# A chunkwise mLSTM scan: stabiliser rows brought in by DMA instead of by TensorE, one minimum for four heads

## The chip, the cores and the metric

The kernel runs on one core of one Trainium2 chip. The metric is the device time of one execution in microseconds (us); the median of three runs of the kernel before is 2629.45 us.

## The reference, cut to what matters

The program is a two-layer encoder trunk (attention and a Hyena operator, then a bidirectional mLSTM, each followed by a mixture of experts) on 1024 positions of width 1024, all in float32. The change lies in the mLSTM of the second layer. It has 4 heads, a forward and a backward scan, chunks of 128 positions; q and k have 128 components a head, v has 256.

```python
def step(carry, inp):                       # one chunk of one head and direction
    c_st, n_st, m_st = carry
    qj, kj, vj, lij, lfj = inp
    bcum = jnp.cumsum(lfj, axis=-1)
    dmat = bcum[..., :, None] - bcum[..., None, :] + lij[..., None, :]
    dmat = jnp.where(mask, dmat, -jnp.inf)
    inter = bcum + m_st[..., None]
    m_t = jnp.maximum(inter, jnp.max(dmat, axis=-1))
    w_intra = jnp.exp(dmat - m_t[..., None])
    w_inter = jnp.exp(inter - m_t)
    sc = jnp.einsum('bgtd,bgsd->bgts', qj, kj) * w_intra
    num = (w_inter[..., None] * jnp.einsum('bgtd,bgde->bgte', qj, c_st)
           + jnp.einsum('bgts,bgse->bgte', sc, vj))
    den = w_inter * jnp.einsum('bgtd,bgd->bgt', qj, n_st) + jnp.sum(sc, axis=-1)
    h = num / jnp.maximum(jnp.abs(den), jnp.exp(-m_t))[..., None]
    ...                                     # the state c, n, m is carried on with kw
```

With A = log_i - bcum (one value per source position s) and M the running maximum of A within the chunk and of the carried one, dmat - m_t is A[s] - M[t]: a column plus a row, masked.

## The kernel before, in words

Every stage of the program ("phase") is a block in which each engine has its own instruction list, with counting semaphores between them, and a barrier of all engines at its end. Four stages matter here.

`ml_gates` (from line 2582) projects the output gate in 16 steps of 24 matmuls on TensorE, and beside that works out the gate rows: 36 partitions (forward heads in rows 0 to 3, backward ones in rows 32 to 35, already reversed in time), 1024 positions. Its `turn_rows` (line 2626) turns five such rows (A, WI, ENM, KW and NEGM = -M) into columns with 40 small transposes, `finish` reverses the backward ones with a matmul against a flip matrix (line 2632), and VectorE copies them to `cols` and `colb`. `ml_project_qk` (line 2773) projects q and k. Weights come in chunks of 2 MB into a ring of three slots in SBUF (`refill`, `load_chunk`), issued by SyncE (SP) when a slot is free; `ml_project_qk` loads the last chunk of the output projection and then the first expert's matrix, chunk S_MOE1.

`ml_scan` (from line 2877) goes through 64 units: 8 chunks, in each 4 forward and then 4 backward heads. For chunk index c > 0 the carried state takes part; the first 32 units also compute and keep k.q, which the second 32 reuse (the other direction needs the same products); the first 56 update the state; units 32 on add their result to what the other direction stored. In the order of the engines' lists, for unit u:

- TensorE, `scores(u+2)`: k.q (line 2917, only u < 32); then the row -M spread over all 128 partitions, as a matmul of the broadcast column `col(4)` with the identity (line 2919); then the inter-chunk product of q with the state (line 2925), into one bank, QB. `values(u)`: the weighted scores with v (line 2934) and the keys with v for the state (line 2940). Each is one float32 matmul, which the profile shows as two.
- ScalarE: `inter(u+1)` scales the inter-chunk product into `t1`, of three buffers (line 2969); the copy of k.q (line 2990); the exponential (line 2993); `scaled(u-4)` divides by the denominator (line 2977).
- VectorE: `exponent(u+1)` takes the spread row, adds the column A and bounds by the mask's table (0 where allowed, -1e30 elsewhere), line 3034; `weigh(u)` multiplies the exponential by k.q (line 3044); `finish(u-1)` adds the two products (line 3059, 3062 in chunk 0), updates the state (line 3066, 3071) and, for an odd unit, makes the denominators of two heads with three tiny instructions (lines 3079, 3082, 3088).
- GpSimd: `kw(u)` scales the keys (line 3016); the addition to the stored result (line 3007).

The waits that set this order:

```python
if u >= 3:                                   # scores(u): three banks
    pe.wait_ge(e_ok, u - 2)
    if u - 3 < FIRST:
        pe.wait_ge(kept, u - 2)
...
if u - 2 * MH >= 3:                          # inter(u), three buffers t1
    act.wait_ge(num_ok, u - 2)
...
for u in range(UNITS):                       # VectorE
    if u + 1 < UNITS:
        exponent(u + 1)
    weigh(u)
    if u:
        finish(u - 1)
```

Before the first unit the keys of all chunks are turned by TensorE, and ScalarE and VectorE copy them out by turns (lines 2983, 3092). After the scan comes the output projection with the router (`out_route`).

Of the kernel before, what the change touches and what calls it, by code (L numbers as in the profile page):

```python
# [7 lines left out]
F32 = mybir.dt.float32  # L8
F32R = mybir.dt.float32r
I32 = mybir.dt.int32  # L10
ALU = mybir.AluOpType
# [3 lines left out]
P = 128  # L15
D = 1024
T = 1024
NT = T // P
# [58 lines left out]
def build(nc, I, out):  # L77
    ctx = ExitStack()
    with ctx:
# [38 lines left out]
        so_d = nc.dram_tensor("sigmoid_o_scratch", (T, D), F32).ap()  # L118

# [2462 lines left out]
        def ml_gates(xnH, cols, colb, apr):  # L2582

            (proj, evac, staged0, staged1, w_high, w_rest, w_used,
             bias_in, shifted, sized, expd, logd, ready, powered, turned, moved, flipped, diag_ok,
             chain) = take(19)
            staged = (staged0, staged1)
            with ExitStack() as st:
# [23 lines left out]
                with nc.Block() as block:  # L2612
                    @block.sync
                    def _(sp):
                        sp.dma_start(gb[:], I["ml_gate_b"]).then_inc(bias_in, 16)
                        refill(sp, C0, C0 + CHUNKS, proj, NT)

                    @block.tensor
                    def _(pe):
                        def turn_rows():  # L2620
                            pe.wait_ge(powered, 3)
                            pe.wait_ge(ready, 1)
                            for n in range(5 * NT):
                                q, c = divmod(n, NT)
                                row = (A, WI, ENM, KW, NEGM)[q]
# [4 lines left out]
                        def finish():  # L2630
                            pe.wait_ge(moved, 3)
                            nc.tensor.matmul(psum[:, 7, 0:160], flip[:], cols[:, :, :, 32:36],
# [65 lines left out]
                    def _(dve):  # L2698
# [50 lines left out]
                        V.tensor_scalar(NEGM, M, -1.0, None, ALU.mult).then_inc(ready, 1)  # L2749
# [7 lines left out]
                        for b in range(3):  # L2757
                            n = min(14, 5 * NT - 14 * b) * GROWS
# [4 lines left out]
                        step(V.tensor_copy(colb[:], psum[:, 7, 0:160].rearrange("p (q c h) -> p q c h", q=5, c=NT)))  # L2763
# [113 lines left out]
        def ml_scan(qkT, kn, vA, cols, colb, apr, hs):  # L2877
            (s_ok, qc_ok, v_ok, cc_ok, e_ok, w_ok, scw_ok, t_ok, num_ok, h_ok, c_ok, kw_ok, den_ok,
             chain, recip_ok, kept, scaled_ok, added_ok, k_turned, k_lo, k_hi) = take(21)
            with ExitStack() as st:  # L2880
                C = sb(st, "ml_state", [P, 2 * MH, MVA])
                small = sb(st, "ml_small", [P, 4, 2, P])
                e0, wT, scw, kw = (small[:, n] for n in range(4))
# [6 lines left out]
                SB, QB = (0, 1, 3), 2  # L2890
# [14 lines left out]
                with nc.Block() as block:  # L2905
                    @block.tensor
                    def _(pe):
                        def scores(u):
                            c, d, h, gi, n, col = unit(u)
                            b = SB[u % 3]  # L2910
# [357 lines left out]
```

## Time and profile before

| | us |
|---|---|
| runs | 2629.45, 2623.35, 2631.92; median 2629.45 |
| profiled execution | 2623.78 |
| its span, first to last instruction | 2622.0 |
| busy over the span | TensorE 91%, VectorE 70%, ScalarE 55%, GpSimd 18% |
| `ml_scan` in it | about 1713.2 to 1831.9, 118.7 us or 4.5% of the span |

A row of the timeline gives start, duration, engine, line, operation, what it writes and reads, its shape and how many instructions were merged; in brackets, how long the engine had been idle before and what ended that. PE is TensorE, PEld its loading of weights, DVE VectorE, ACT ScalarE, POOL GpSimd, SPq the queue of SyncE. Names are those of the allocated tiles: `ml_small` holds exponent, weights, weighted scores and scaled keys, `ml_inter` is t1, `ml_num` num, `ml_state` the state, `ml_kq` the kept products, `ml_k` the turned keys, `ml_den` the denominators.

### The profile page before, as it was taken

To read this page: it belongs to the slowest core of one execution; us is meant where nothing else is said; L and a number is where in the kernel's file an instruction comes from. 1 tells how busy PE (TensorE), PEld (TensorE's weight loads), DVE (VectorE), ACT (ScalarE), POOL (GpSimd) and SP (SyncE) were. 2 spreads that over 40 slices of the span, in tenths; PEclk is the share of its full clock that TensorE was granted. 3 is DMA by queue.
4 is the path that set the end of the run, shared out by engine and by line. 5 is a ranking of instruction groups with operands and counts; after the bars stand their busy time and mean duration, and the time that the engine had idled before them with its cause. 6 is when DMAs were issued, how large, how long until landed. Compare 5 with 4: busy or idle time off the path is not lost. (4 is left out here: it accounts for less than half of the span.)

```text
span 2622.0 us, 32575 instructions
## 1 busy us (share of the span) xinstructions
PE 2392.4 (91%) x11612; PEld 1966.8 (75%) x11612; DVE 1826.0 (70%) x2101; ACT 1452.5 (55%) x1777; POOL 482.4 (18%) x431
## 2 busy tenths in 40 slices
PE   7989989796978999999986998988896999999996
PEld 6768877585867888888875876876785888888884
DVE  6848856578447988998963141378637989888982
ACT  6438842322217887888863241256424878877872
POOL 0001100100002333333320000036201333323321
PEclk9989999897988999999997999999897999999999
DMA  5110011111237999999993121000425999999996
GB/s 178 47 52 1 1 48 37 73 33 35 112 124 286 392 380 382 391 388 382 388 382 124 59 84 59 33 33 8 159 108 209 381 382 379 364 386 373 385 389 246
DMA packets 85913, 542.32 MB, mean 207 GB/s; under 512 B 18997, under 2 KB 22678, under 8 KB 59831
## 3 DMA queue, kind: packets, MB, share of 16 engines
q1 hardware_dynamic: 64358, 502.93, 48.9%
q0 software_dynamic: 19008, 33.61, 5.2%
q10 hardware_dynamic: 2448, 4.46, 0.5%
q8 instruction: 62, 1.02, 0.2%
q14 instruction: 37, 0.30, 0.0%
HBM read 521.52 MB, written 55.05 MB: 220 GB/s over the span
## 5 line engine op out<-in xcount | busy, mean ns | idle before, releaser
L2280 DVE TENSOR_TENSOR wL<-ring,wH 128x2048 fp32r<-128x2048 f32 x384 | 869.4, 2288 | 134.5 <-ACT wH L2216 128.2
L2216 ACT CAST wH<-ring 128x2048 fp32r<-128x2048 f32 x384 | 730.1, 1911 | 194.2 <-DMA ring<-in_moe_w 138.7
L2102 PE MATMUL psum<-wH,xgH 128*128 128x512 f32 x1024 | 407.6, 398 | 14.4 <-DVE xgL L2280 14.4
L2104 PE MATMUL psum<-wH,xgL 128*128 128x512 f32 x1024 | 401.2, 392 | 0.0
L2110 PE MATMUL psum<-wL,xgH 128*128 128x512 f32 x1024 | 275.8, 391 | 0.0
L2102 PEld LDWEIGHTS psum<-wH,xgH 128*128 128x128 f32 x1024 | 193.5, 189 | 57.1 <-DVE xgL L2280 13.1
L2110 PEld LDWEIGHTS psum<-wL,xgH 128*128 128x128 f32 x1024 | 193.2, 189 | 40.8
L2104 PEld LDWEIGHTS psum<-wH,xgL 128*128 128x128 f32 x1024 | 193.7, 189 | 38.4
L2102 PE MATMUL psum<-wH,hidH 128*128 128x512 f32 x512 | 206.0, 402 | 3.9 <-DVE hidL L2280 3.9
L2104 PE MATMUL psum<-wH,hidL 128*128 128x512 f32 x512 | 200.2, 391 | 0.0
L2020 POOL COPY gidx<-slots 128x1 int32 (+1 forms) x60 | 61.1, 1019 | 497.5 <-PE psum L2119 497.5
L2110 PE MATMUL psum<-wL,hidH 128*128 128x512 f32 x512 | 137.7, 391 | 0.0
L200 PE MATMUL psum<-xn_high,ring_rest 128*128 128x512 f32 x320 | 127.2, 397 | 0.0
L198 PE MATMUL psum<-w_high_route_rest,y_high_route 128*128 128x512 f32 x256 | 105.7, 413 | 12.6 <-DVE ring_rest L193 12.1
L2102 PEld LDWEIGHTS psum<-wH,hidH 128*128 128x128 f32 x512 | 96.5, 189 | 23.2 <-DVE hidL L2280 4.4
L2110 PEld LDWEIGHTS psum<-wL,hidH 128*128 128x128 f32 x512 | 96.7, 189 | 20.2
L2104 PEld LDWEIGHTS psum<-wH,hidL 128*128 128x128 f32 x512 | 96.7, 189 | 18.3
L2034 POOL COPY yidx<-slots 128x1 int32 (+1 forms) x64 | 97.1, 1517 | 56.9 <-DMA out<-y,yidx 33.6
L199 PE MATMUL psum<-ring_rest,y_high_route 128*128 128x512 f32 x256 | 102.4, 400 | 0.0
L200 PE MATMUL psum<-w_high_route_rest,y_rest_route 128*128 128x512 f32 x256 | 102.1, 399 | 0.0
L199 PE MATMUL psum<-ring_rest,xn_high 128*128 128x512 f32 x256 | 102.1, 399 | 0.0
L2227 ACT ACTIVATE y<-psum,slot_gate 128x1024 f32<-128x1024 f32 x64 | 71.5, 1117 | 49.2 <-PE psum L2110 49.0
(429 smaller groups left out, 4657.3 us busy)
## 6 DMA issues: line engine op xcount, KB each, us to landing
ring<-in_moe_w SPq DMA_DIRECT2D x192, 2048.0 KB
ring<-in_ev_w_in SPq DMA_DIRECT2D x6, 2048.0 KB
xnT<-in_moe_w SPq DMA_DIRECT2D x6, 2048.0 KB, 14.3
ring<-in_od_w_in SPq DMA_DIRECT2D x6, 2048.0 KB
xn_scratch<-xn_route SPq DMA_DIRECT2D x16, 512.0 KB, 2.6
ow<-in_moe_w SPq DMA_DIRECT2D x3, 2048.0 KB, 22.8
v_att<-in_x SPq DMA_DIRECT2D x8, 512.0 KB, 3.9
ring<-in_ev_w_out SPq DMA_DIRECT2D x2, 2048.0 KB
```

The lines of the kernel that those rows point to most:

```text
L198: nc.tensor.matmul(dst, lhs[0], rhs[0], start=start, stop=False)
L199: nc.tensor.matmul(dst, lhs[0], rhs[1], start=False, stop=False)
L200: return nc.tensor.matmul(dst, lhs[1], rhs[0], start=False, stop=stop)
L2020: nc.gpsimd.tensor_copy(idx[:, b:b + 1], slots[:, bass.ds(e, 1)]).then_inc(idx_ok, 1)
L2034: nc.gpsimd.tensor_copy(yidx[:, b:b + 1], slots[:, bass.ds(e, 1)]).then_inc(yidx_ok, 1)
L2102: nc.tensor.matmul(psum[:, bank, :], xh[:, k, :], w3[0][:, n, cols], start=(half == 0 and n == 0), stop=False)
L2104: nc.tensor.matmul(psum[:, bank, :], xl[:, k, :], w3[0][:, n, cols], start=False, stop=False)
L2110: ins = nc.tensor.matmul(psum[:, bank, :], xh[:, k, :], w3[1][:, n, cols], start=False, stop=(half == 1 and n == len(ks) - 1))
L2216: nc.scalar.copy(half_of(wH, b, e, c, half), raw(e, c, half)).then_inc(w_high, 1)
L2227: nc.scalar.activation(y[:, b, :], psum[:, 5:7, :].rearrange("p a b -> p (a b)"), ACT.Copy, scale=slot_gate[:, bass.ds(e, 1)]).then_inc(y_ ...
L2280: return nc.vector.tensor_tensor(out, whole, high.bitcast(F32), ALU.subtract)
```

## The change

The spread row no longer comes from TensorE. `ml_gates` turns four rows instead of five (32 transposes, and 128 columns instead of 160 in the flip matmul); VectorE writes the backward rows of -M once more, reversed, and SyncE stores the 8 rows to a DRAM scratch. In `ml_scan` SyncE reads them back, per chunk and direction 4 heads by 128 positions broadcast to 128 partitions (256 KB in SBUF), 16 such transfers into two buffers that lie in ring slot S_MOE1 % 3; the load of chunk S_MOE1 moves from the end of `ml_project_qk` to the scan, behind the last use of the rows. VectorE takes one minimum of four heads' rows against the mask's table (now +1e30 where allowed), with both inputs in SBUF, once for four units; ScalarE adds the column A as the bias of its exponential. The k.q product has two banks instead of three, the inter-chunk product two instead of one.

```diff
@@ ml_gates
-                        refill(sp, C0, C0 + CHUNKS, proj, NT)
+                        refill(sp, C0, C0 + CHUNKS - 1, proj, NT)
+                        sp.wait_ge(natural, 2)
+                        sp.dma_start(rows_d[0:MH, :], NEGM[0:MH, :]).then_inc(rows_out, 16)
+                        sp.dma_start(rows_d[MH:2 * MH, :], A[32:32 + MH, :]).then_inc(rows_out, 16)
+                        sp.wait_ge(proj, NT * CHUNKS)
+                        load_chunk(sp, C0 + CHUNKS - 1 + RING)
+                        sp.wait_ge(rows_out, 32)
...
-                            for n in range(5 * NT):
+                            for n in range(4 * NT):
...
+                        dve.wait_ge(natural, 1)
+                        V.tensor_copy(A[32:32 + MH, :], NEGM[32:32 + MH, ::-1]).then_inc(natural, 1)
@@ ml_project_qk
-                        refill(sp, C0, C0 + 2, proj, 4)
+                        refill(sp, C0, C0 + 1, proj, 4)
@@ ml_scan
-                SB, QB = (0, 1, 3), 2
+                SB, QB = (0, 1), (2, 3)
+                wide_rows = ring[:, S_MOE1 % RING, 0:4 * MH * P].rearrange("p (b g t) -> p b g t", b=2, g=2 * MH)
...
+                    @block.sync
+                    def _(sp):
+                        for c in range(NT):
+                            if c >= 2:
+                                sp.wait_ge(e_ok, 2 * (c - 1))
+                            for d in range(2):
+                                n = NT - 1 - c if d else c
+                                sp.dma_start(wide_rows[:, c % 2, MH * d:MH * d + MH, :],
+                                             rows_d[MH * d:MH * d + MH, n * P:(n + 1) * P].partition_broadcast(P)
+                                             ).then_inc(rows_in[c % 2], 16)
+                        sp.wait_ge(e_ok, 2 * NT)
+                        load_chunk(sp, S_MOE1)
...
-                            if u >= 3:
-                                pe.wait_ge(e_ok, u - 2)
-                                if u - 3 < FIRST:
-                                    pe.wait_ge(kept, u - 2)
                             if u < FIRST:
-                                nc.tensor.matmul(psum[:, b, 0:P], qkT[:, 4 + h, t], qkT[:, h, t], start=True, stop=True)
-
-                            nc.tensor.matmul(psum[:, b, P:2 * P], col(4).broadcast_to([P, P]), ident[:],
-                                             start=True, stop=True).then_inc(s_ok, 1)
+                                if u >= 2:
+                                    pe.wait_ge(kept, u - 1)
+                                nc.tensor.matmul(psum[:, SB[u % 2], 0:P], qkT[:, 4 + h, t], qkT[:, h, t], start=True,
+                                                 stop=True).then_inc(s_ok, 1)
                             if c:
                                 pe.wait_ge(c_ok, u - 2 * MH + 1)
-                                if u - 2 * MH >= 1:
-                                    pe.wait_ge(t_ok, u - 2 * MH)
+                                if u - 2 * MH >= 2:
+                                    pe.wait_ge(t_ok, u - 2 * MH - 1)
...
-                            act.wait_ge(e_ok, u + 1)
                             if u < FIRST:
+                                act.wait_ge(s_ok, u + 1)
+                                nc.scalar.copy(kq[:, n, h, :], psum[:, SB[u % 2], 0:P]).then_inc(kept, 1)
+                            act.wait_ge(e_ok, u // MH + 1)
                             if u >= 2:
                                 act.wait_ge(scw_ok, u - 1)
-                            nc.scalar.activation(wT[:, u % 2, :], e0[:, u % 2, :], ACT.Exp).then_inc(w_ok, 1)
+                            nc.scalar.activation(wT[:, u % 2, :], e0[:, (u // MH) % 2, h, :], ACT.Exp, bias=col(0)
+                                                 ).then_inc(w_ok, 1)
...
+                        def bound(g):
+                            c, d = divmod(g, 2)
+                            dve.wait_ge(rows_in[c % 2], 32 * (c // 2 + 1))
+                            if g >= 2:
+                                dve.wait_ge(w_ok, MH * (g - 1))
+                            V.tensor_tensor(e0[:, g % 2, :, :], wide_rows[:, c % 2, MH * d:MH * d + MH, :],
+                                            (cap_b if d else cap_f)[:].unsqueeze(1).broadcast_to([P, MH, P]), ALU.min
+                                            ).then_inc(e_ok, 1)
...
+                        bound(0)
                         for m in range(1, NT, 2):
                             dve.wait_ge(k_turned, m + 1)
                             V.tensor_copy(kn[:, key_chunk(m), :], psum[:, 4 + m % 4, :]).then_inc(k_hi, 1)
-                        exponent(0)
                         for u in range(UNITS):
-                            if u + 1 < UNITS:
-                                exponent(u + 1)
+                            if u % MH == 1 and u + MH < UNITS:
+                                bound(u // MH + 1)
                             weigh(u)
```

## Rows read from the trace of the kernel before

**Rows 1.** By stretch: length, busy PE, PEld, DVE, ACT, POOL; clock, DMA share, GB/s.

```profile
1722.00:1736.00 14.00, 13.27 (x78) 12.14 (x79) 12.05 (x48) 7.83 (x29) 5.21 (x9) 1.00 0.01 2
1736.00:1782.00 46.00, 46.00 (x257) 40.76 (x256) 39.23 (x147) 32.31 (x104) 18.70 (x27) 1.00 0.00 1
1782.00:1816.00 34.00, 33.43 (x166) 27.01 (x165) 31.82 (x113) 21.79 (x61) 25.91 (x40) 1.00 0.01 2
```

**Rows 2.** Waits in the last of these stretches: who waited for whom, us, times, longest.

```profile
ACT ml_inter L2969 <- DVE ml_num L3059: 8.1, 10, 1.3
```

**Rows 3.** Timeline of two units of chunk 2, parts of it.

```profile
1758.78 0.60 PE L2925 MATMUL psum<-ml_state,ml_qkT 128*128 128x257 f32 x2
...
1759.42 0.48 ACT L2969 ACTIVATE ml_inter<-psum,ml_cols 128x257 f32<-128x257 f32 x1 [0.51 <-PE psum L2925]
...
1759.79 0.26 ACT L2990 COPY ml_kq<-psum 128x128 f32<-128x128 f32 x1
...
1760.30 0.39 PE L2919 MATMUL psum<-ident,ml_cols 128*128 128x128 f32 x2
...
1760.53 0.60 PE L2925 MATMUL psum<-ml_state,ml_qkT 128*128 128x257 f32 x2
...
1762.04 0.29 DVE L3044 SCALAR_TENSOR_TENSOR ml_small<-ml_kq,ml_small 128x128 f32<-128x128 f32 x1 [0.47 <-ACT ml_small L2993]
...
1763.44 0.35 DVE L3034 SCALAR_TENSOR_TENSOR ml_small<-psum,ml_cols,cap_f 128x128 f32<-128x128 f32 x1
```

**Rows 4.** Timeline of two units of chunk 5, parts of it.

```profile
1797.55 0.28 DVE L3044 SCALAR_TENSOR_TENSOR ml_small<-ml_kq,ml_small 128x128 f32<-128x128 f32 x1
...
1798.26 0.48 ACT L2969 ACTIVATE ml_inter<-psum,ml_colb 128x257 f32<-128x257 f32 x1 [0.80 <-DVE ml_num L3059]
...
1798.97 0.29 DVE L3044 SCALAR_TENSOR_TENSOR ml_small<-ml_kq,ml_small 128x128 f32<-128x128 f32 x1
...
1800.52 0.35 DVE L3034 SCALAR_TENSOR_TENSOR ml_small<-psum,ml_cols,cap_f 128x128 f32<-128x128 f32 x1
...
1800.79 0.28 DVE L3044 SCALAR_TENSOR_TENSOR ml_small<-ml_kq,ml_small 128x128 f32<-128x128 f32 x1
```

**Rows 5.** Timeline of VectorE: the weighing of units 8, 32 and 56.

```profile
1734.04 0.29 DVE L3044 SCALAR_TENSOR_TENSOR ml_small<-ml_kq,ml_small 128x128 f32<-128x128 f32 x1 [0.53 <-ACT ml_small L2993]
...
1775.86 0.29 DVE L3044 SCALAR_TENSOR_TENSOR ml_small<-ml_kq,ml_small 128x128 f32<-128x128 f32 x1
...
1815.33 0.29 DVE L3044 SCALAR_TENSOR_TENSOR ml_small<-ml_kq,ml_small 128x128 f32<-128x128 f32 x1
```

**Rows 6.** One VectorE instruction of `ml_gates` with two SBUF inputs (ns least/median/most).

```profile
L2736 DVE TENSOR_TENSOR gate_rows<-gate_rows x1: 1216/1216/1216, 1527.4 to 1527.4; 36x1024 f32<-36x1024 f32 x1
```

**Rows 7.** Groups of ScalarE instructions without and with a per-partition operand, 512 elements.

```profile
L1605 ACT ACTIVATE hy_abs<-xnT 128x512 f32<-128x512 f32 x16 | 9.2, 619 | 1.8 <-DVE xnT L1639 1.8
L1594 ACT ACTIVATE hy_decay<-hy_delta,hy_tneg 128x512 f32<-128x512 f32 x8 | 5.6, 714 | 0.0
```

**Rows 8.** Timeline of TensorE in `ml_gates`: the transposes, and what follows them.

```profile
1557.53 2.68 PE L2626 MATMUL psum<-ident,gate_rows 36*128 36x36 f32 x40
1560.14 0.50 PE L198 MATMUL psum<-w_high_o,xn_high 128*128 128x512 f32 x1
```

**Rows 9.** Timeline of the start of `ml_scan`.

```profile
1713.24 5.01 PEld L2949 LDWEIGHTS psum<-ident,ml_qkT 128*128 128x128 f32 x32 [6.98 <-issue]
...
1719.33 0.30 PEld L2917 LDWEIGHTS psum<-ml_qkT 128*128 128x128 f32 x2 [1.08 <-ACT ml_k L2983]
```

**Rows 10.** DMA issues of broadcast rows: KB each, us from issue to landing.

```profile
g_att<-in_ev_subln SPq DMA_DIRECT2D x1, 256.0 KB, 3.2
h_gain_route<-in_od_out_norm SPq DMA_DIRECT2D x1, 512.0 KB, 5.2
```

**Rows 11.** Timeline of the scan's end: GpSimd's addition and a denominator of VectorE.

```profile
1828.85 0.64 POOL L3007 TENSOR_TENSOR xnT<-xnT,ml_num 128x256 f32<-128x256 f32 x1
1829.03 0.48 DVE L3079 SCALAR_TENSOR_TENSOR ml_den<-ml_num 128x2 f32<-128x2 f32 x1
```

More of the change, by code:

```diff
@@ L2584, in ml_gates @@
             (proj, evac, staged0, staged1, w_high, w_rest, w_used,
-             bias_in, shifted, sized, expd, logd, ready, powered, turned, moved, flipped, diag_ok,
-             chain) = take(19)
+             bias_in, shifted, sized, expd, logd, powered, turned, moved, flipped, diag_ok,
+             chain, natural, rows_out) = take(20)
             staged = (staged0, staged1)
@@ L2621, in turn_rows @@
                             pe.wait_ge(powered, 3)
-                            pe.wait_ge(ready, 1)
-                            for n in range(5 * NT):
+                            for n in range(4 * NT):
                                 q, c = divmod(n, NT)
-                                row = (A, WI, ENM, KW, NEGM)[q]
+                                row = (A, WI, ENM, KW)[q]
                                 last = nc.tensor.transpose(psum[:, 4 + n // 14, (n % 14) * GROWS:(n % 14 + 1) * GROWS],
@@ L2631, in finish @@
                             pe.wait_ge(moved, 3)
-                            nc.tensor.matmul(psum[:, 7, 0:160], flip[:], cols[:, :, :, 32:36],
+                            nc.tensor.matmul(psum[:, 7, 0:128], flip[:], cols[:, :, :, 32:36],
                                              start=True, stop=True).then_inc(flipped, 1)
@@ L2878, in ml_scan @@
             (s_ok, qc_ok, v_ok, cc_ok, e_ok, w_ok, scw_ok, t_ok, num_ok, h_ok, c_ok, kw_ok, den_ok,
-             chain, recip_ok, kept, scaled_ok, added_ok, k_turned, k_lo, k_hi) = take(21)
+             chain, recip_ok, kept, scaled_ok, added_ok, k_turned, k_lo, k_hi, rows_in0, rows_in1) = take(23)
+            rows_in = (rows_in0, rows_in1)
             with ExitStack() as st:
                 C = sb(st, "ml_state", [P, 2 * MH, MVA])
-                small = sb(st, "ml_small", [P, 4, 2, P])
-                e0, wT, scw, kw = (small[:, n] for n in range(4))
+                small = sb(st, "ml_small", [P, 3, 2, P])
+                wT, scw, kw = (small[:, n] for n in range(3))
+                e0 = sb(st, "ml_bound", [P, 2, MH, P])
                 t1 = sb(st, "ml_inter", [P, 3, MVA])
@@ L2986, in _ @@
                                 inter(u + 1)
-                            act.wait_ge(e_ok, u + 1)
+                            c, d, h, gi, n, col = unit(u)
                             if u < FIRST:
-                                c, d, h, gi, n, col = unit(u)
-                                nc.scalar.copy(kq[:, n, h, :], psum[:, SB[u % 3], 0:P]).then_inc(kept, 1)
+                                act.wait_ge(s_ok, u + 1)
+                                nc.scalar.copy(kq[:, n, h, :], psum[:, SB[u % 2], 0:P]).then_inc(kept, 1)
+                            act.wait_ge(e_ok, u // MH + 1)
                             if u >= 2:
                                 act.wait_ge(scw_ok, u - 1)
-                            nc.scalar.activation(wT[:, u % 2, :], e0[:, u % 2, :], ACT.Exp).then_inc(w_ok, 1)
+                            nc.scalar.activation(wT[:, u % 2, :], e0[:, (u // MH) % 2, h, :], ACT.Exp, bias=col(0)
+                                                 ).then_inc(w_ok, 1)
                             if u >= 4:
@@ L3026, in _ @@
                         did = Tally(chain)
-                        def exponent(u):
-                            c, d, h, gi, n, col = unit(u)
-                            dve.wait_ge(s_ok, u + 1)
-                            if u >= 2:
-                                dve.wait_ge(w_ok, u - 1)
-                            V.scalar_tensor_tensor(out=e0[:, u % 2, :], in0=psum[:, SB[u % 3], P:2 * P], scalar=col(0),
-                                                   in1=(cap_b if d else cap_f)[:], op0=ALU.add, op1=ALU.min
-                                                   ).then_inc(e_ok, 1)
+                        def bound(g):
[6 more added lines that the diff above has]
+                                            ).then_inc(e_ok, 1)
                         def weigh(u):
```

20 lines of the change are left out of this document (10 added, 10 removed).

## The prediction

> **What bounds the kernel now.** The page gives shares over the whole span, so I first cut out the stage by the busy times of its stretches [rows 1]. The scan is 118.7 us. In chunks 1 to 3 TensorE is busy for the whole 46 us, VectorE 39.23. In chunks 4 to 6, which have no k.q product, TensorE shows 33.43 of 34 us and VectorE 31.82: either could be the bound there, and a busy TensorE can be one that merely stretches over short gaps. So I went to the timeline for the distance between successive weighings, the one instruction of VectorE that every unit has. Units 8 to 32 take 1775.86 - 1734.04 = 41.82 us, 1.743 a unit; units 32 to 56 take 1815.33 - 1775.86 = 39.47 us, 1.645 a unit [rows 5].
>
> In chunks 1 to 3 one inter-chunk product starts 1.75 us behind the other (1758.78, 1760.53) and TensorE does not wait: it is the bound, and the spreading matmul takes 0.23 us of each unit (1760.30 to 1760.53) [rows 3].
>
> In chunks 4 to 6 there are two kinds of gap [rows 4]. The **short** one (1797.55 to 1798.97, 1.42 us) is a loop through two engines: weighing of u, sum of u-1, ScalarE's inter-chunk scaling of u+2 (0.71 after the weighing; it waited 0.80 for the sum, since t1 has three buffers), exponential of u+1, next weighing (another 0.71). The waits confirm it: ScalarE waited for the sum ten times in the stretch, 8.1 us [rows 2]. The **long** one (1798.97 to 1800.79, 1.82 us) is VectorE's own work with the three denominator instructions in it. A pair must average 2 x 1.645 = 3.29, so long gaps average 3.29 - 1.42 = 1.87.
>
> **The change, part by part.**
>
> *Exponent removed.* Its start-to-start share of VectorE is 0.27 us (1800.52 to 1800.79) [rows 4]. It is on the path only in long gaps. In short ones the loop sets the time, and the exponent isn't in the loop.
>
> *Bound added, 16 times.* The nearest row is an instruction with two SBUF inputs and 1024 elements, 1.216 us [rows 6]; the weighing, also with two, has 128 elements and takes 0.28 [rows 4]. Between them 0.00104 us an element, so 0.68 for 512. Queued instructions overlap by about 0.08 (the exponent lasts 0.35 and its follower starts after 0.27), so 0.60 in a queue. Below, 4 x 0.27 = 1.08 removed for 0.60 added looks like a gain of 0.12 a unit; but the bound stands in front of the weighing of u = 4k+1, behind `finish(4k-1)`, that is always in a long gap.
>
> *Bias on the exponential.* Of two 512-element groups the one with a per-partition operand takes 714 ns, the other 619 [rows 7]: 0.095 more for each of 64 exponentials, and this one **is** in the loop.
>
> *Chunks 4 to 6.* Short gap 1.42 + 0.095 = 1.51. Long gap 1.87 - 0.27 = 1.60. Long gap with bound 1.60 + 0.60 = 2.20. Four units: 1.51 + 1.60 + 1.51 + 2.20 = 6.82, before 4 x 1.645 = 6.58: +0.24, six times, +1.4 us.
>
> *The spreading matmul removed, chunks 1 to 3.* TensorE alone would need 1.743 - 0.23 = 1.51 a unit. But the k.q product goes from three banks to two: `scores(u+2)` now waits for ScalarE's copy of k.q of u, one unit later than before. ScalarE does that copy behind its inter-chunk scaling of u+1. This closes a loop: inter-chunk product of u+1 to scaling 0.64 (1758.78 to 1759.42), scaling to copy 0.37 (to 1759.79), copy 0.26, signal 0.05 (product's end 1759.38 to ScalarE's 1759.42) [rows 3], then weights and k.q product before the next inter-chunk product. For those I take 0.11 for the first weights (two loads in 0.30 at the first k.q product [rows 9]) plus 0.22 as the spreading one of the same shape. The sum is 1.65 a unit. Bounds: 1.51 if this wait never bites, 1.743 if the stall costs TensorE more at restart; I take 1.65. The gap with the bound: without the exponent the weighing could follow after 1.40 (1762.04 to 1763.44 [rows 3]), with the bound after 2.00. That is 0.35 over 1.65, of which about 0.12 is slack of the scaling (2.29 by the product, 2.17 by the sum), so 0.23 stays. Four units: 6.60 + 0.23 = 6.83, taken as 6.9; before 6.97. Six times: -0.4 us.
>
> *Chunk 0.* VectorE is busy 12.05 of 14 us [rows 1], no state product, no scaling in the loop: here its work counts. 8 x 0.27 - 2 x 0.60 = 1.0: -1.0 us.
>
> *Chunk 7.* One bound (+0.60), up to three exponents in long gaps (-0.81), four short gaps by +0.095: about +0.1 to +0.2, taken as 0.
>
> *Second inter-chunk bank.* It removes a wait that shows nowhere: TensorE's inter-chunk product does not wait in the rows read. 0; if a slower scaling (+0.095) crowds it, the bank only hides that.
>
> *Sharing with GpSimd.* Its addition and VectorE's two-input instruction collide: with the addition at 1828.85 to 1829.49 a two-element instruction lasted 0.48 and ended at 1829.51 [rows 11]. GpSimd is busy 25.91 of 34 us in chunks 4 to 6 [rows 1]; each of some 7 bounds there may wait from 0 to 0.64 us. I take 0.15 each: +1 us; range 0 to 4.5.
>
> *Start of the scan.* Two 256 KB transfers of rows are issued when the stage starts (1713.24 [rows 9], the second some 0.4 later). The nearest broadcast of that size landed after 3.2 us, one of 512 KB after 5.2 [rows 10]; the descriptors here are 512-byte rows. So landing at 1716.9, between 1716.0 and 1719. VectorE waits for it **ahead** of its four key copies, and TensorE's key transposes wait for those copies. Bound until 1717.5, four copies of about 0.6, two of them held by the transposes: first k.q product at 1720.1 instead of 1719.33 [rows 9], +0.8. Back come 0.6 us, because ScalarE's first copy no longer waits for the spreading matmul and exponent. Net +0.2; -0.6 to +2.
>
> *`ml_gates`.* 40 transposes take 1560.14 - 1557.53 = 2.61 us of a TensorE without gaps [rows 8]; 8 fewer are 0.5, the smaller flip matmul nothing measurable: -0.5 us. The reversed copy on VectorE (four partitions, 1024 elements) and the two row stores lie beside five more projection steps; SyncE's next weight load waited for the last step before too. If that cover failed, under 2 us.
>
> *S_MOE1 moved.* 2 MB that were loaded before the scan go out after the last bound (unit 57, some 10 us before the end) and even at twice the 5.2 us of the 512 KB broadcast [rows 10] they land about when the output stage begins. Its first use is many steps later. 0; should it slide into that stage's own loads, up to 2 us.
>
> **Sum**: -0.5 + 0.2 - 1.0 - 0.4 + 1.4 + 1.0 = +0.7 us on the profiled execution's 2623.78. The median of the runs is 5.7 above that execution, so the forecast is 2629.45 + 0.7, rounded to 2630. About 0.3% (7.9 us) is what a measurement of this kernel can tell from no change; so "no change".
>
> **The rivals.**
>
> *A: the relief is real.* The second bank of k.q costs nothing and the loops are looser than I read them. Then chunks 1 to 3 gain 24 x 0.23 = 5.5, the other 40 units 40 x (0.27 - 0.15) = 4.8, with the -0.5 of `ml_gates` 10.8 in all: 2618.7. For it: TensorE is gapless there. Against it: short gaps repeat at 1.42 and cannot shrink by this change. 11 in 100.
>
> *B: slower, through the port that VectorE and GpSimd share.* Each bound of the second half meets an addition or a key scaling, waits for it (0.64), holds GpSimd for 0.6, and the denominators behind are late again: 1.1 a bound for 8 bounds, with the rest of the sum (-0.3) about +8.5: 2638. It decides against the forecast when the bound's mean duration in chunks 4 to 6 passes 1.4 us instead of 0.68. The Trainium skill states it as a rule (SBUF — State Buffer, "Who interferes with whom"): a VectorE instruction with two SBUF inputs contends with a GpSimd instruction that reads SBUF, and whoever issues first holds the pair for the whole instruction. By that rule the exponent before, with one input in PSUM, was free of it and the bound is not; the trace agrees in the 0.48 us of the denominator. Against B: GpSimd has gaps, and the bound comes behind the denominators, which have already waited it out. 13 in 100 with other ways to lose.
>
> *C: late rows.* The first rows land only at 1722 or later: +4 to +6, 2635; still no measurable change. It counts within the 76.
>
> **Chances.** Forecast with C 0.76, A and the like 0.11 faster, B and the like 0.13 slower. The range 2620 to 2638 takes in the unknown terms (-3 for the k.q loop, +3.5 for the port, +2 for the start, +2 for loads), the 4 us by which medians move, and the near edges of A and B.
>
> **What the profile would show.** No L2919-like matmul in the scan; short gaps of weighing at 1.51 in chunks 4 to 6; long ones near 1.6, every second of them near 2.2; units in chunks 1 to 3 at about 1.7, with TensorE's k.q product waiting for ScalarE's copy, a wait absent before; the exponential 0.1 us longer than before. The stage still 118 to 120 us. Wrong would be: units at 1.51 in chunks 1 to 3 (A), bounds above 1 us (B), VectorE idle at the start beyond 1720 (C).

## The result, and the profile after

The changed kernel takes 2635.16 us, median of 20 runs; the kernel before 2626.64 us, median of 20. The ratio is 1.0029, 95% interval 1.0021 to 1.0038: slower by 0.29%. The interval leaves out 1, so the loss is real, though small; it lies just inside the 0.3% that the prediction called no change. The forecast was +0.7 us over a median of three runs that itself lay 2.8 above the median of twenty, so 2630 is 3.4 us above the latter; 8.5 us were measured.

The loss is in the scan. From the first key transpose to the first gain load of the output stage it took 119.9 us before (1713.27 to 1833.2) and 131.2 us after (1716.42 to 1847.6). The rest of the profiled execution is 3.2 us later at the scan's start and 2.5 us quicker after it; other profiled executions of the same code outside the scan differ by as much, so I read nothing into these.

The starts of successive weighings give the scan by chunk, in us (the last interval of chunk 7 ends at the last weighing):

| | first transpose to first weighing | chunk 0 | chunks 1 to 3 | chunks 4 to 6 | chunk 7 |
|---|---|---|---|---|---|
| before | 9.1 | 11.65 | 41.8 | 39.5 | 12.2 |
| after | 12.9 | 13.6 | 44.2 | 43.2 | 11.6 |
| forecast change | +0.2 | -1.0 | -0.4 | +2.4 with the port | 0 |
| measured change | +3.8 | +2.0 | +2.4 | +3.7 | -0.6 |

Added up, +1.2 us was forecast for the scan and +11.3 measured.

The busy times of stretches of the changed kernel: the start, the first units, chunks 1 to 3, chunks 4 to 6. Columns as in the first line.

```profile
core 0: us, PE busy (x) PEld busy (x) DVE busy (x) ACT busy (x) POOL busy (x), PEclk, DMA share, GB/s
1716.00:1722.00 6.00, 4.50 (x20) 4.13 (x20) 0.00 (x0) 1.76 (x3) 0.00 (x0) 0.55 0.46 134
1729.00:1737.00 8.00, 7.31 (x26) 6.21 (x26) 5.35 (x17) 3.78 (x14) 1.99 (x4) 0.62 0.31 67
1744.00:1787.00 43.00, 42.23 (x184) 27.61 (x183) 32.89 (x110) 30.79 (x94) 16.77 (x23) 1.00 0.13 37
1788.00:1831.00 43.00, 36.79 (x145) 25.20 (x145) 36.16 (x115) 27.76 (x72) 28.91 (x43) 1.00 0.10 26
```

Against [rows 1] TensorE has lost its full share in chunks 4 to 6: 36.79 of 43 us. In chunks 1 to 3 it still shows 42.23 of 43, though it is no longer the bound there; only its weight loads tell, which fall from 40.76 of 46 to 27.61 of 43. In the first 8 us from the first weighing on, most of chunk 0, its granted clock is 0.62 of full speed, so for most of that time at 1.2 instead of 2.4 GHz; before it was 1.00. The key transposes ran at the lower level in both kernels (0.55 here, 0.50 from 1713 to 1716 before).

The start of the scan in the changed kernel's timeline answers to [rows 9]:

```profile
1716.37 2.03 SPq L2929 DMA_DIRECT2D ring<-scan_rows_scratch  x4
1716.42 4.50 PE L2973 MATMUL psum<-ident,ml_qkT 128*128 128x128 f32 x20 [6.58 <-PEq L110]
...
1722.44 0.69 DVE L3061 TENSOR_TENSOR ml_bound<-ring,cap_f 128x512 f32<-128x512 f32 x1 [8.06 <-DMA ring<-scan_rows_scratch]
1723.05 1.28 DVE L3120 COPY ml_k<-psum 128x512 f32<-128x512 f32 x2
1723.79 1.86 PE L2973 MATMUL psum<-ident,ml_qkT 128*128 128x128 f32 x12 [2.87 <-DVE ml_k L3120]
...
1726.53 1.92 PE L2943 MATMUL psum<-ml_qkT 128*128 128x128 f32 x6 [0.88 <-DVE ml_k L3120]
```

SyncE issues four transfers at once, those of chunks 0 and 1, and not two as the prediction has it. The first pair, which the first minimum needs, has landed 6.0 us after the start. VectorE sits idle for 8.06 us, TensorE stops for 2.87 us with 20 of 32 transposes done, and the first k.q product starts 10.1 us after the first transpose instead of 6.1.

Three weighings of chunk 6 and what lies between them, in parts, answer to [rows 4]:

```profile
1815.70 0.29 DVE L3071 SCALAR_TENSOR_TENSOR ml_small<-ml_kq,ml_small 128x128 f32<-128x128 f32 x1 [0.50 <-ACT ml_small L3018]
...
1817.36 0.69 DVE L3061 TENSOR_TENSOR ml_bound<-ring,cap_b 128x512 f32<-128x512 f32 x1
1817.66 0.88 POOL L3033 TENSOR_TENSOR xnT<-xnT,ml_num 128x256 f32<-128x256 f32 x1 [0.20 <-ACT ml_num L3001]
1817.96 0.73 DVE L3071 SCALAR_TENSOR_TENSOR ml_small<-ml_kq,ml_small 128x128 f32<-128x128 f32 x1
...
1819.12 0.48 ACT L2993 ACTIVATE ml_inter<-psum,ml_cols 128x257 f32<-128x257 f32 x1 [1.54 <-DVE ml_num L3086]
1819.49 0.39 ACT L3018 ACTIVATE ml_small<-ml_bound,ml_cols 128x128 f32<-128x128 f32 x1
...
1819.91 0.29 DVE L3071 SCALAR_TENSOR_TENSOR ml_small<-ml_kq,ml_small 128x128 f32<-128x128 f32 x1 [0.50 <-ACT ml_small L3018]
```

The long gap with the minimum is 2.26 us (1815.70 to 1817.96; forecast 2.20), and the minimum lasts 0.69. But the weighing behind it lasts 0.73 instead of 0.29: GpSimd's addition, itself lengthened behind the minimum (0.88 instead of 0.64), ends at 1818.54, and the weighing ends 0.15 later. That the weighing waits for the addition is read from these times here; experiment 7 shows it. So the gap after it is 1.95 instead of the forecast 1.51. The other two are 1.58 and 1.52. Four units take 7.31; the forecast was 6.82.

The last unit of chunk 2, in parts, up to the first weighing of chunk 3, answers to [rows 3]:

```profile
1770.63 0.60 POOL L3042 TENSOR_SCALAR ml_small<-ml_k,ml_cols 128x128 f32<-128x128 f32 x1 [1.19 <-PE psum L2964]
1770.74 0.41 DVE L3071 SCALAR_TENSOR_TENSOR ml_small<-ml_kq,ml_small 128x128 f32<-128x128 f32 x1 [0.20 <-ACT ml_small L3018]
...
1771.07 0.41 DVE L3086 TENSOR_TENSOR ml_num<-ml_inter,psum 128x257 f32<-128x257 f32 x1
...
1771.57 0.48 ACT L2993 ACTIVATE ml_inter<-psum,ml_cols 128x257 f32<-128x257 f32 x1 [0.47 <-DVE ml_num L3086]
...
1771.95 0.26 ACT L3014 COPY ml_kq<-psum 128x128 f32<-128x128 f32 x1
1772.09 0.41 ACT L3018 ACTIVATE ml_small<-ml_bound,ml_cols 128x128 f32<-128x128 f32 x1
...
1772.54 0.40 DVE L3071 SCALAR_TENSOR_TENSOR ml_small<-ml_kq,ml_small 128x128 f32<-128x128 f32 x1 [0.67 <-ACT ml_small L3018]
```

The chain is the loop through t1, now here too: sum 0.33 after the weighing, scaling at 0.83, copy at 1.21, exponential at 1.35, next weighing at 1.80. GpSimd's key scaling starts 0.11 us ahead of the weighing, and the weighing lasts 0.41 instead of 0.28 (that the one causes the other is read from their times); behind a weighing of 0.28 the gap is 1.67. A chunk has two gaps with a minimum in them, of 2.12, so four units mostly take 2.12 + 1.67 + 1.80 + 1.80 = 7.4 us. The waits of chunks 1 to 3 name the loop first among VectorE, ScalarE and TensorE (us in total, times, longest):

```profile
ACT ml_inter L2993 <- DVE ml_num L3086: 11.4, 21, 0.8
DVE ml_small L3071 <- ACT ml_small L3018: 8.8, 16, 1.0
PEld psum L2943 <- ACT ml_kq L3014: 6.8, 20, 0.6
```

### The profile page after: what moved, and what is told of

The parts are those of the page before. It is cut to its first block and busy times, and to the rows that moved or that the text cites. A ratio compares the mean times of both kernels' runs of the same rounds, so it can differ in the third digit from the quotient of the medians.

```text
span 2633.9 us, 32223 instructions
## 1 busy us (share of the span) xinstructions
PE 2394.6 (91%) x11476; PEld 1950.2 (74%) x11476; DVE 1821.5 (69%) x2054; ACT 1456.5 (55%) x1777; POOL 486.4 (18%) x431
## 5 line engine op out<-in xcount | busy, mean ns | idle before, releaser
L2103 PE MATMUL psum<-wH,xgH 128*128 128x512 f32 x1024 | 407.9, 398 | 12.7 <-DVE xgL L2281 12.6
L2035 POOL COPY yidx<-slots 128x1 int32 (+1 forms) x64 | 89.3, 1395 | 66.6 <-DMA out<-y,yidx 34.2
L621 DVE TENSOR_REDUCE neg_max<-psum 128x1 f32<-128x1024 f32 x64 | 75.4, 1220 | 32.0 <-PE psum L545 32.0
```

The costliest lines, as they stand in the source:

```text
L621: nc.vector.tensor_reduce(nmx[:, i % 2, c:c + 1], pair(u), AX, ALU.max, negate=True).then_inc(max_neg, 1)
L2035: nc.gpsimd.tensor_copy(yidx[:, b:b + 1], slots[:, bass.ds(e, 1)]).then_inc(yidx_ok, 1)
L2103: nc.tensor.matmul(psum[:, bank, :], xh[:, k, :], w3[0][:, n, cols], start=(half == 0 and n == 0), stop=False)
```

## The experiments

Ratios are to the kernel before, run on the same chip, with their 95% intervals. In the short diffs the old line stands first. A list of gaps is a list of distances between starts of weighings.

**1. The first minimum behind the key copies (late_first_bound).**

```diff
-                        bound(0)
                         for m in range(1, NT, 2):
...
+                        bound(0)
```

> Edit: VectorE makes the first minimum behind its four key copies instead of ahead of them. Theory (start): in the changed kernel the rows landed 6.0 us after the stage's start, VectorE sat 8.1 us, the key copies and the k.q product came late, TensorE idled and its clock was at the lower level again in chunk 0; that is 3.8 us before the first weighing (12.9 us from the first key transpose instead of 9.2) and about 2 us in chunk 0 (13.6 instead of 11.65). So here the first weighing should come 9 to 9.5 us after the first transpose, chunk 0 take 11 to 11.7, the later chunks stay at 14.7 a chunk; the whole 5 to 6 us faster than the changed kernel, about 1 to 3 us slower than before. Rival (the start matters little, the clock of chunk 0 falls anyway because TensorE idles for the exponential's table): 3.8 us come back and chunk 0 stays at 13.6.

Ratio 1.0021 (1.0006 to 1.0036). The first weighing comes 8.65 us after the first transpose (1709.11 to 1717.76), half a microsecond sooner than before the change. Nothing waits for the rows any more, with nothing to spare: they land when the key copies end. Chunk 0 takes 12.65, between the two expectations; the clock is at its lower level from 1719.2 to 1722.6, after TensorE had waited for 1.55 us (1716.56 to 1718.11) while ScalarE loaded the exponential's table and made its first exponential. The scan takes 125.9 us. So the start cost 4.3 us directly, and some of chunk 0 with it. That figure moves from execution to execution: the seven profiled executions with the minimum ahead of the copies have 12.9 to 13.9 us to the first weighing, the changed kernel's own being the shortest, and the kernel before has 9.1 in one and 10.3 in the other (experiment 5), with a mean clock of 0.83 and 0.73 over that stretch.

**2. The other minima in the short gap (short_gap_bound).**

```diff
-                            if u % MH == 1 and u + MH < UNITS:
+                            if u % MH == 2 and u + MH < UNITS:
```

> Edit: the minimum stands before the weighing of unit 4k+2 instead of 4k+1, that is behind a finish without denominators. Theory (place): VectorE has 0.92 us of work in that gap and waits for the loop through t1 till 1.51, so 0.60 more fits; in chunks 4 to 6 four gaps should be 1.55, 1.6, 1.55, 1.6 = 6.3 us instead of 7.32, chunk 5 about 12.6 instead of 14.63; chunks 1 to 3 at 1.70 to 1.80 a unit, 13.6 to 14.2. About 7 us less than the changed kernel over the stage. Rival (port shared with GpSimd): the place does not matter, because the weighing behind the minimum still finds GpSimd holding the port, lasts 0.73 and makes a gap of 1.95; then chunk 5 is 13.9 or more.

Ratio 1.0015 (1.0000 to 1.0031). Chunk 5 falls from 14.63 to 12.66, its gaps are 1.68, 1.54, 1.59, 1.52: the minimum costs next to nothing where VectorE waits for the loop anyway. Chunks 1 to 3 are 14.1, 14.6 and 14.2. The place theory holds; the place also keeps the minimum and the addition apart, so this run does not separate the two. The scan of the profiled execution takes 124.7 us; its start was slow, with the first weighing after 13.9 us.

**3. The mask read from PSUM (mask_in_psum).**

```diff
+                        did(V.tensor_copy(psum[:, 3, 0:P], cap_f[:]))
+                        did(V.tensor_copy(psum[:, 3, P:2 * P], cap_b[:]))
...
-                                            (cap_b if d else cap_f)[:].unsqueeze(1).broadcast_to([P, MH, P]), ALU.min
+                                            psum[:, 3, P * d:P * d + P].unsqueeze(1).broadcast_to([P, MH, P]), ALU.min
```

> Edit: the two mask tables are copied to a PSUM bank at the stage's start and the minimum reads its mask there, so that it has one input in SBUF; the inter-chunk product goes back to one bank to make room. Port theory: GpSimd's addition is no longer held up by the minimum (0.88 back to 0.64 or 0.79), the weighing behind it lasts 0.29 instead of 0.73, and the gap after it falls from 1.95 to 1.51: chunk 5 from 14.63 to 13.7, chunks 1 to 3 from 14.7 to about 14.2 (weighing 0.29 instead of 0.40). Some 4 us in all. Rival (the 1.95 gap comes from the loop restarted late, not from the port): gaps stay 2.26 and 1.95.

Ratio 1.0037 (1.0022 to 1.0051). Chunk 5 falls to 14.14, half of what was expected: the addition lasts 0.64 again instead of 0.88, the weighing behind the minimum 0.50 instead of 0.73, and the gap after it is 1.72 instead of 1.95. The rival is wrong, but so is my 1.51: the weighing has two SBUF inputs of its own and still meets the addition. Chunks 1 to 3 stay at 14.6 to 14.9, where it is the weighing, not the minimum, that collides. The scan as a whole shows no gain (131.4 us): here the first weighing comes 13.9 us after the first transpose instead of 12.9. That is not the price of the two added copies, since experiment 4, without them, has 13.9 too.

**4. Three k.q banks again (three_kq_banks).**

```diff
-                SB, QB = (0, 1), (2, 3)
+                SB, QB = (0, 1, 3), (2,)
```

> Edit: the k.q product has three banks as before, the inter-chunk product one. Theory (two banks): TensorE waited 7 us for ScalarE's copy of k.q in chunks 1 to 3; without that wait these chunks should go from 14.7 to 14.0 each (the loop through t1, 0.65 to 0.75 us to the scaling and then copy and exponential, is then the bound at about 1.62 to 1.70 a unit), chunks 4 to 6 stay. About 2 us less. Rival (that wait only takes the place of the one for the weighing; the loop through t1 at 1.67 to 1.80 is the real bound): chunks 1 to 3 stay within 0.2 us of 14.7. The single inter-chunk bank should cost nothing by both.

Ratio 1.0046 (1.0029 to 1.0062); the scan takes 132.0 us. Chunks 1 to 3 are 14.61, 14.97 and 14.61, to 0.02 us those of the changed kernel. My step is refuted: the wait for the copy of k.q (7.0 us in chunks 1 to 3 of the changed kernel) is gone, and TensorE's weight loads wait for the weighing instead, 10.8 us where it was 6.9. The slower loop stood behind the wait. Two inter-chunk banks instead of one bring nothing either.

**5. Four buffers t1 (four_t1), and the same on the kernel before (before_four_t1).**

```diff
-                t1 = sb(st, "ml_inter", [P, 3, MVA])
+                t1 = sb(st, "ml_inter", [P, 4, MVA])
...
-                                if u - 2 * MH >= 3:
-                                    act.wait_ge(num_ok, u - 2)
+                                if u - 2 * MH >= 4:
+                                    act.wait_ge(num_ok, u - 3)
```

> Edit on the changed kernel: four buffers t1 instead of three (to make room the bounded exponents lie in the ring slot too, and chunk S_MOE1 is loaded when the last exponential is done). Loop theory: the short gaps (1.51 in chunks 4 to 6, 1.80 in chunks 1 to 3) are set by ScalarE's scaling waiting for the sum that frees t1. With a fourth buffer chunk 5 should fall from 14.63 to 12.0 to 12.8 (VectorE's own work: 0.92, 1.6, 0.92, 2.2 and what the shared port adds), chunks 1 to 3 from 14.7 to 13.2 to 13.9 (then the two k.q banks are the bound at 1.65). Rival (the gaps are set by the chain product, scaling, exponential, weighing, values through TensorE): at most 0.3 us a chunk change.

> Edit on the kernel before, nothing else of the change: four buffers t1. Loop theory: chunks 4 to 6 fall from 13.15 to 12.2 each (TensorE's 1.525 a unit and VectorE's 3.05 a pair are then the bound together), chunks 1 to 3 stay at 13.9 since TensorE is the bound there: about 3 us, 0.1%. Rival: no chunk moves.

On the changed kernel: ratio 0.9999 (0.9982 to 1.0016), chunks 1 to 3 39.9 instead of 44.2, chunk 5 13.48. The short gaps are 1.37 and 1.30 instead of 1.95 and 1.52, so the loop was their cause. The chunk stays above my 12.8, since the gap with the minimum is as long as ever (2.26) and the other long one grew from 1.59 to 1.81, where the weighing now lasts 0.58. On the kernel before: ratio 0.9979 (0.9965 to 0.9994), chunks 5 and 6 12.62 instead of 13.13, chunks 1 to 3 41.6 instead of 41.8. One buffer of 1 KB a partition is worth 0.2% without the rest of the change. I had expected 12.2; the long gaps are 1.92 and 1.77 (1.92 and 1.82 before), and of the short ones only one came down, to 1.18; the other went from 1.41 to 1.44, and what holds it was not followed.

**6. No column (no_column).**

```diff
-                            nc.scalar.activation(wT[:, u % 2, :], e0[:, (u // MH) % 2, h, :], ACT.Exp, bias=col(0)
+                            nc.scalar.activation(wT[:, u % 2, :], e0[:, (u // MH) % 2, h, :], ACT.Exp
```

> Edit on the changed kernel: the exponential has no bias, so that the column A is left out of the exponent. Bias theory: the exponential lasts 0.30 instead of 0.40 and, being in the loop, takes 0.09 off each gap that the loop sets: chunk 5 from 14.63 to about 14.2, chunks 1 to 3 from 14.7 to 14.0; 3 to 4 us in the stage. Rival (the operand is fetched in the shadow of the instruction before): 0.40 in the profile, but the starts keep their distance and no chunk moves by more than 0.2.

This kernel leaves the column A out of the exponent. The values that reach the experts' routing are others, and the whole takes 2714.78 us; only the scan can be read. The exponential lasts 0.31 instead of 0.40. The short gaps in chunks 4 to 6 are 1.42 instead of 1.51, the one after the minimum 1.86 instead of 1.95, and the long ones do not move (2.25, 1.58): 0.09 in each gap that the loop sets. In chunks 1 to 3 the 1.80 become 1.65, more than the bias, as the weighing then starts ahead of the key scaling or with it, and lasts 0.29 to 0.31.

**7. The exponential in PSUM for the second half (weights_in_psum).**

```diff
+                def weight(u):
+                    return wT[:, u % 2, :] if u < FIRST else psum[:, u % 2, 0:P]
...
-                            V.scalar_tensor_tensor(out=scw[:, u % 2, :], in0=kq[:, n, h, :],
-                                                   scalar=KSCALE, in1=wT[:, u % 2, :], op0=ALU.mult, op1=ALU.mult
+                            V.scalar_tensor_tensor(out=scw[:, u % 2, :], in0=weight(u),
+                                                   scalar=KSCALE, in1=kq[:, n, h, :], op0=ALU.mult, op1=ALU.mult
```

> Edit on the changed kernel: for units 32 on ScalarE writes the exponential into one of the two k.q banks of PSUM, idle by then, so that the weighing has one input in SBUF instead of two; the minimum keeps two. Port theory: the gap behind the minimum, 1.95 with a weighing of 0.73, falls to 1.5 to 1.6 because the weighing no longer waits for GpSimd; chunks 5 and 6 go from 14.6 to 13.7 to 13.9 each, chunks 1 to 3 stay at 14.6 to 15.0. Rival (the 1.95 is the time that the loop needs to restart behind the late weighing): weighing 0.35, gap still 1.9, chunk 5 at 14.5.

One execution took 2629.91 us. VectorE's timeline, chunk 5:

```profile
1806.96 0.69 DVE L3064 TENSOR_TENSOR ml_bound<-ring,cap_f 128x512 f32<-128x512 f32 x1
1807.57 0.28 DVE L3074 SCALAR_TENSOR_TENSOR ml_small<-psum,ml_kq 128x128 f32<-128x128 f32 x1
1809.05 0.29 DVE L3074 SCALAR_TENSOR_TENSOR ml_small<-psum,ml_kq 128x128 f32<-128x128 f32 x1 [0.47 <-ACT psum L3021]
1810.66 0.29 DVE L3074 SCALAR_TENSOR_TENSOR ml_small<-psum,ml_kq 128x128 f32<-128x128 f32 x1
1812.14 0.29 DVE L3074 SCALAR_TENSOR_TENSOR ml_small<-psum,ml_kq 128x128 f32<-128x128 f32 x1 [0.47 <-ACT psum L3021]
```

The weighing behind the minimum lasts 0.28, the gap after it is 1.48 (1807.57 to 1809.05), and chunk 5 takes 13.70. GpSimd's addition still lasts 0.90 beside it. The instruction, its size, its place and the minimum before it are the same; one input has moved out of SBUF, and the two inputs have changed places in the call. So the weighing's 0.45 us comes from its second SBUF input beside GpSimd's work, and not from a loop restarted late. The exponential itself is 0.03 shorter (0.36 instead of 0.39), which is why the other short gaps are 1.48 instead of 1.51. Chunks 1 to 3, untouched by the edit, stay at 14.6 to 15.0.

**8. Start and place together (start_and_place):** the edits of 1 and 2.

> Edit on the changed kernel: first minimum behind the key copies and the others in the short gap; buffers and banks as changed. If start and place add up: first weighing 8.7 us after the first key transpose, chunk 0 about 12.2, chunks 1 to 3 14.2, chunks 4 to 6 12.6, the stage about 120 us, level with before (ratio 0.998 to 1.001). Rival (they overlap, as both are about VectorE's order): over 122 us.

Ratio 0.9992 (0.9978 to 1.0005), the scan 117.7 us, a little better than expected. Chunk 0 takes 10.95: in this run the first units have the full clock,

```profile
1717.00:1721.00 4.00, 1.58 (x10) 0.99 (x8) 1.76 (x4) 2.77 (x6) 1.48 (x2) 1.00 0.14 37
1721.00:1731.00 10.00, 9.84 (x48) 8.18 (x49) 9.03 (x33) 5.78 (x19) 4.40 (x7) 1.00 0.26 55
```

(busy times by stretch, columns as above; the second is most of chunk 0), and 11.65 - 10.95 is 0.7 of the 1.0 us that I had forecast for chunk 0, though with the minima in another place. TensorE's waits at the start are the same as in experiment 1 (0.88 and 1.55 us), and there the clock fell for 3.4 us of chunk 0: what decides it is not shown.

**9. A version that beats both (combined):** 1, 2, the banks of 4 and the buffers of 5.

> All together on the changed kernel: first minimum behind the key copies, the others in the short gap, three k.q banks and one inter-chunk bank, four buffers t1. If start, place, loop and banks are the causes, the first weighing comes 8.7 us after the first key transpose, chunk 0 takes 12 to 12.7, chunks 1 to 3 about 12.5 each (TensorE's 1.51 a unit), chunks 4 to 6 about 11.8 to 12.4 each: the stage 112 to 115 us instead of 131 (before: 120), the kernel 5 to 8 us faster than before, ratio 0.997 to 0.998. Rival (the shared port takes what the buffers give): chunks 4 to 6 at 13 or more and the kernel level with before.

2615.72 us, median of 12; ratio 0.9962 (0.9948 to 0.9976). The scan takes 111.1 us. Chunks 1 to 3 take 37.5; chunks 4 to 6 12.2, 12.1 and 13.1. The first weighing comes 8.6 us after the first transpose. The timelines of VectorE and GpSimd still show the two at odds: a key scaling of 1.16 us, instead of 0.60, beside the minimum.

```profile
1793.88 0.70 DVE L3061 TENSOR_TENSOR ring<-ring,cap_b 128x512 f32<-128x512 f32 x1
1794.01 1.16 POOL L3042 TENSOR_SCALAR ml_small<-ml_k,ml_cols 128x128 f32<-128x128 f32 x1
```

**10. The same with the port relieved (combined_port):** 1, 2, the buffers of 5, two k.q banks, the mask of 3 and the exponential of 7.

> The combined version (first minimum behind the copies, others in the short gap, four t1), with two k.q banks and one inter-chunk bank, the mask read from the bank that this frees and, from unit 32 on, the exponential from the k.q banks: no VectorE instruction of the scan but the denominators has two inputs in SBUF in its second half. Port theory: chunks 5 and 6 from 12.1 to 13.1 in the combined version to about 11.5 each, chunks 1 to 3 at 12.5 to 13.3 (two banks: 1.57 to 1.65 a unit); ratio to before about 0.996. Rival (VectorE's own work and the sum's wait for GpSimd's addition are the bound): chunks 5 and 6 stay at 12 or more.

2615.47 us, median of 11; ratio 0.9962 (0.9948 to 0.9976), level with 9. Chunks 5 and 6 take 11.9 and 12.0, above the 11.5 of the theory and at the rival's 12: this run does not decide between them. Chunks 4 to 6 take 1.9 us less than in 9, but chunks 1 to 3 take 1.4 more, and this execution's start and chunk 0 are slow (first weighing after 10.0, chunk 0 13.3, its mean clock 0.76). Chunks 1 and 2 now go at 1.645 a unit, 13.2 a chunk, with TensorE waiting for the copy of k.q in each unit:

```profile
1752.62 0.49 PE L2946 MATMUL psum<-ml_qkT 128*128 128x128 f32 x2
...
1752.95 0.60 PE L2952 MATMUL psum<-ml_state,ml_qkT 128*128 128x257 f32 x2
...
1753.59 0.47 ACT L2996 ACTIVATE ml_inter<-psum,ml_cols 128x257 f32<-128x257 f32 x1 [0.32 <-PE psum L2952]
...
1753.96 0.26 ACT L3017 COPY ml_kq<-psum 128x128 f32<-128x128 f32 x1
...
1754.27 0.30 PEld L2946 LDWEIGHTS psum<-ml_qkT 128*128 128x128 f32 x2 [0.26 <-ACT ml_kq L3017]
...
1754.60 0.60 PE L2952 MATMUL psum<-ml_state,ml_qkT 128*128 128x257 f32 x2
```

Product 1752.95, scaling 1753.59, copy 1753.96, weights 1754.27, next product 1754.60: the loop of the two banks, 1.65 as forecast, and visible only once the loop through t1 is out of its way. With three banks (9) the same chunks take 12.2 to 12.7.

## Why the prediction was right, and where not

The time lies in the range and the change is within what the prediction called no change, but that is in good part luck. The stage was to stay at 118 to 120 us and grew by 11 us, against +1.2 forecast; it is 4.5% of the whole, and the range was 18 us wide. The sign held, and so did the reasons why the removed matmul and the removed exponent bring so little: short gaps cannot shrink, they grew by the bias (0.09, experiment 6), and the minimum stood in the long gap (2.26 against 2.20, experiment 2). Of the signs named in advance the gaps of 1.51, 1.6 and 2.2 in chunks 4 to 6, TensorE's wait for the copy of k.q and the longer exponential came; the unit of 1.7 in chunks 1 to 3 was 1.84. By steps:

- *Exponent removed, bound added.* Right: 0.69 us each, 1.58 instead of 1.82 or 1.92 in a long gap without a minimum.
- *Bias.* Right, 0.09 on the path in each short gap.
- *Sharing with GpSimd.* The mechanism was right and the place wrong. I looked for the price in the minimum's own duration, and named 1.4 us of it as the point from which rival B decides. The minimum never grew (0.69). It delayed GpSimd's addition, and the addition then held up the next instruction with two SBUF inputs, the weighing, by 0.44 and with it the loop. 0.15 a bound was mis-sized; the gap after it measured 0.44 over the forecast, six times from chunk 4 on: 2.6 us, against the 1.0 forecast. The Trainium skill (SBUF — State Buffer, "Who interferes with whom") states that a VectorE instruction with two SBUF inputs contends with a GpSimd instruction that reads SBUF. The runs agree: with the minimum's mask in PSUM the addition took 0.64 instead of 0.88 (experiment 3), with the exponential in PSUM the weighing took 0.28 instead of 0.73 (experiment 7). B named the right mechanism for chunks 4 to 6, but its 1.1 us a bound was too much.
- *Chunks 1 to 3.* Two steps failed. First, the bound: the two-bank loop is 1.65, as experiment 10 shows, but the loop through t1 is slower, at 0.71 + 0.37 + 0.15 + 0.44 = 1.67. I had seen that loop in chunks 4 to 6 and did not write it down with the copy of k.q in it for chunks 1 to 3. With the matmul gone TensorE stopped being the bound, and the 0.23 us a unit that it saved came back as waits. Second, the sharing with GpSimd was priced at nothing here. Wherever the key scaling starts 0.10 to 0.11 us ahead of the weighing, the weighing lasts 0.40 or 0.41, and so two of four gaps are 1.80. The gap with the minimum is 2.12: the 2.00 of the prediction and again 0.12 of a lengthened weighing (2.01 where that lasts 0.29), so that the 0.12 of slack that I took off is not there. Of the 0.57 us by which four units exceed the 6.83 of the sum, three lengthened weighings are about 0.38, the slack 0.12 and the slower loop 0.06. -0.4 was forecast, +2.4 measured.
- *Start of the scan.* The step that failed by most. I took 3.2 us for a 256 KB broadcast from one row; of these, with rows of 512 bytes, the first two took 4.7 and 5.6 from issue to landing, the sixteen 5.1 in the median, and the first pair had landed 6.0 us after the start. That is just past the end of my range for the landing and short of rival C's, but my range for the cost ended at +2; measured were +3.8, close to C's +4, and experiment 1 returns 4.3.
- *Chunk 0.* Forecast -1.0, measured +2.0, with the clock at its lower level for most of it (0.62 from 1729 to 1737), a cost that the sum does not have. At the upper level it is -0.7 (experiment 8). In all seven profiled executions with the minimum ahead of the key copies TensorE had stopped for 2.6 to 3.4 us, the mean clock of chunk 0 was 0.77 to 0.83 and the chunk took 13.05 to 13.95 us. That the stop lowers the clock is likely and not shown: without it chunk 0 had 1.00, 0.87, 0.86 and 0.76 (experiments 8, 1, 9 and 10).
- *Chunk 7.* Forecast 0, measured -0.6: the gap with the minimum and the one behind it grew by 0.9 together (2.11 and 1.95 for 1.77 and 1.41), but four gaps of 1.77 to 1.94 without a minimum are now 1.43 to 1.53.
- *`ml_gates`.* The transposes took 2.10 us (1561.29 to 1563.39) instead of 2.61, the 0.5 forecast. In the stage as a whole it cannot be seen: from its first load to that of the next stage it took 105.2 us, before 104.9, and in the other profiled executions of this code 102.7 to 105.8.
- *S_MOE1 moved.* 0; issued at 1832.54, some 15 us before the output stage's loads, nobody waited for it.

What stays open is why two broadcasts of 512-byte rows need 6 us. It is not that four go out together: the later pairs, alone in the queue, took 4.4 to 5.0 and 5.1 to 6.3 us from issue to landing. An earlier issue was not tried, only the removal from VectorE's path.

## What to carry to other kernels

Before an operation is taken off a saturated engine, write down every loop that closes through a buffer count, with all its links, for each stretch that has different links; the engine's share says only that it is busy, and the next loop may be 4% behind. Extra work goes where the engine waits for such a loop: the same two minima cost 2 us a chunk in one place, with what they set off, and next to nothing in another (chunk 5: 14.63 and 12.66 us). When an operand moves from PSUM to SBUF on VectorE while GpSimd works beside it, look at the instruction **behind** it for the price.

## What the runs showed of the hardware

- A VectorE instruction with two SBUF inputs and a GpSimd instruction delay each other: a 128-element weighing took 0.73 us instead of 0.28, a key scaling 1.10 to 1.16 instead of 0.60. With one of the two inputs in PSUM the weighing took 0.28 in the same place.
- A per-partition bias costs ScalarE 0.09 us an instruction (0.40 against 0.31), and all of it shows in the distance of starts.
- A stage's start can cost twice: 2.87 us of stopped transposes, and then a clock of 0.62 over most of chunk 0, which took 13.6 us; with the rows off the path, the minimum in the short gap and the clock at 1.00 it took 10.95. The link between the two is not shown.
- The same code at a stage's start took 9.1 us in one execution and 10.3 in another, with a mean clock of 0.83 and 0.73: a difference of 1 us there is not a result.
